# Stacked half-precision products for the sample states, chunk states ahead of the exponent differences, and key copies ahead of the weight split in a hybrid decoder step

## What is computed

```python
def hgrn2_block(s0, q, k, v, log_f):
    ...
    s_new = jnp.exp(b_last)[..., None] * s0 + jnp.einsum('bshk,bshv->bhkv', k * jnp.exp(b_last[:, None] - b), v)
    return s_new, o

def retention_block(s0, q, k, v):
    ...
    s_new = jnp.exp(c * log_gamma)[None, :, None, None] * s0 + jnp.einsum('bshk,bshv->bhkv', k * k_dec[None, :, :, None], v)
    return s_new, o
```

## Time and profile before

| | us |
|---|---|
| median of 3 runs | 1739.92 (1738.65 to 1740.34) |
| the profiled execution's own time | 1742.57 |
| its span, first to last instruction | 1741.0 |
| PE busy | 1567.8 (90%) |
| DVE busy | 904.5 (52%) |
| ACT busy | 654.0 (38%) |
| POOL busy | 154.3 (9%) |

### The profile page before, as it was taken

How to read it: one execution, slowest core, us unless ns; L and a number is a source line. 1 busy time by engine, 2 the same in 40 slices (tenths; PEclk the granted TensorE clock), 3 DMA queues, 4 the chain that set the end, 5 groups by cost and what they waited for, 6 DMA issues and landing times.

```text
span 1741.0 us, 31399 instructions
## 1 busy us (share of the span) xinstructions
PE 1567.8 (90%) x12107; PEld 1251.0 (72%) x12107; DVE 904.5 (52%) x1389; ACT 654.0 (38%) x920; POOL 154.3 (9%) x126
## 2 busy tenths in 40 slices
PE   4699999989699999999867999999886999999994
PEld 3477777767578888788755777777765888887883
DVE  4766644444565555533266665444356555553334
ACT  3645523332353334422155452333225443333213
POOL 2111111100200000000030111000002000000002
PEclk8799989988899999999978899999888999999997
DMA  6132222221123332233221224232031223322321
GB/s 192 46 90 77 75 75 75 74 74 55 57 73 97 96 96 77 70 93 95 82 66 51 74 74 111 57 88 78 27 97 48 88 83 96 96 81 74 97 66 51
DMA packets 175035, 138.05 MB, mean 79 GB/s; under 512 B 5064, under 2 KB 169192, under 8 KB 174776
## 3 DMA queue, kind: packets, MB, share of 16 engines
q1 hardware_dynamic: 168192, 113.46, 22.0%
q0 software_dynamic: 5408, 18.60, 3.8%
q10 hardware_dynamic: 1372, 5.16, 0.9%
HBM read 125.12 MB, written 12.07 MB: 79 GB/s over the span
## 4 chain that ended last, share of the span: by engine, by line
PE 77%; DVE 9%; ACT 6%; issue 4%; DVEq 2%; ACTq 1%; DMA 1%; SPq 0%
PE ACC L510 61%; PE SCR L624 2%; PE OT L632 2%; PE SCR L662 1%; ACT WH L830 1%; DVE X L1193 1%; PE OT L684 1%; PE SCR L545 1%; PE SCR L727 1%; DVE Z L1222 1%; DVE Fb L1206 1%; DVE WL L1153 1%; PE OT L600 1%; DVEq L1261 1%; PE OT L599 1%
## 5 line engine op out<-in xcount | busy, mean ns | idle before, releaser
L510 PE MATMUL ACC<-XH,WH 128*128 128x280 f16 x2432 | 502.6, 289 | 70.8 <-DVE XL L1196 43.1
L510 PE MATMUL ACC<-XL,WH 128*128 128x280 f16 x2432 | 502.4, 289 | 0.0
L510 PE MATMUL ACC<-XH,WL 128*128 128x280 f16 x2432 | 501.6, 289 | 0.0
L510 PEld LDWEIGHTS ACC<-XH,WH 128*128 128x128 f16 x2432 | 238.7, 101 | 153.0 <-DVE XL L1196 45.6
L1153 DVE SCALAR_TENSOR_TENSOR WL<-stage,WH 128x2048 f16<-128x2048 f32 (+1 forms) x116 | 245.9, 2120 | 182.0 <-ACT WH L830 170.2
L510 PEld LDWEIGHTS ACC<-XL,WH 128*128 128x128 f16 x2432 | 243.3, 100 | 58.6
L510 PEld LDWEIGHTS ACC<-XH,WL 128*128 128x128 f16 x2432 | 243.3, 100 | 58.0
L830 ACT ACTIVATE WH<-stage 128x2048 f16<-128x2048 f32 (+1 forms) x116 | 204.8, 1766 | 103.7 <-PE ACC L510 86.9
L510 PE MATMUL ACC<-shared,WH 128*128 128x280 f16 x1408 | 225.2, 283 | 0.2
L510 PEld LDWEIGHTS ACC<-shared,WH 128*128 128x128 f16 x1408 | 137.6, 98 | 30.8 <-issue 0.8
L510 PE MATMUL ACC<-shared,WL 128*128 128x280 f16 x704 | 141.5, 283 | 0.0
(11 more groups left out here) (238 smaller groups left out, 1791.4 us busy)
## 6 DMA issues: line engine op xcount, KB each, us to landing
stage<-in_w_in_dram SPq DMA_DIRECT2D x64, 512.0 KB, 5.3
stage<-in_w_a_dram SPq DMA_DIRECT2D x44, 512.0 KB, 4.3
stage<-in_w_b_dram SPq DMA_DIRECT2D x44, 512.0 KB, 4.8
stage<-in_w_down_dram SPq DMA_DIRECT2D x32, 384.0 KB, 3.3
stage<-in_w_down_dram SPq DMA_DIRECT2D x32, 320.0 KB, 3.7
out_dram<-shared POOLq DMA_DIRECT2D x16, 512.0 KB, 3.9
stage<-in_w_o_dram SPq DMA_DIRECT2D x16, 512.0 KB, 3.9
shared<-in_state_hgrn_dram POOLq DMA_DIRECT2D x8, 512.0 KB, 5.7
```

What stands on the lines that cost most here:

```text
L510: last = mm(ACC[:, acc, h, 0:HALF], lhs, x[:, xk + k, h * HALF:(h + 1) * HALF], start=begin, stop=end)
```

## The change

It does three things. First, the sample rows of keys and values are split into a float16 high part and a rest, and the three products high·high, high·rest and rest·high are stacked along the 96 rows of one float16 matmul: the three copies of the 32 sample columns are made ahead of the transposes (a broadcast copy of `KE` on DVE, a second read of the values on ACT), the transposes yield 96 rows, ACT writes all in float16 (`KV3`) and a float32 copy of the values (`VTS`) for the output product, and DVE puts the rest into 32 rows of the keys and 32 of the values (`low_sample_rows`). `VX` has 96 rows in float16. Second, DVE's chunk states (`b()`) come ahead of the exponent differences. Third, in the groups that carry a retention head ACT runs the head's first stage (`a()`) ahead of the weight split, and in the output projection ahead of the output gate.

```diff
-        VX = sb("VX", [TS, DEC_BATCH, P])
-        KVTS = sb("KVTS", [TS, 2, P])
+        VX = sb("VX", [TS3, DEC_BATCH, P], F16)
+        KV3 = sb("KV3", [TS3, 2, P], F16)
+        VTS = sb("VTS", [TS, P])
...
-                pool.wait_ge(tok_ready, hh + 1)
-                nc.gpsimd.tensor_tensor(VX[:, :, :], KVTS[:, 1:2, :].to_broadcast([TS, DEC_BATCH, P]), bcast(seqm[0:TS, :], P),
+                pool.wait_ge(kv_low, hh + 1)
+                nc.gpsimd.tensor_tensor(VX[:, :, :], KV3[:, 1:2, :].to_broadcast([TS3, DEC_BATCH, P]), bcast(seqm[0:TS3, :], P),
                                         ALU.mult).then_inc(vx_ready, 1)
...
-                mm(SCR[:, bank, :], KVTS[:, 0, :], VX[:, 4 * n:4 * n + 4, :].rearrange("p b v -> p (b v)"),
+                mm(SCR[:, bank, :], KV3[:, 0, :], VX[:, 4 * n:4 * n + 4, :].rearrange("p b v -> p (b v)"),
                    start=True, stop=True).then_inc(scr_full, 1)
...
             def read_acc(buf, c, tile, done):
                 act.wait_ge(acc_full, 1 + tile + 1)
-                f(halves(buf[:, 0:T]), ACC[:, c, :, 0:HALF], ACT.Copy, scale=INV_W).then_inc(acc_read[c], 1)
+                last = f(halves(buf[:, 0:T]), ACC[:, c, :, 0:HALF], ACT.Copy, scale=INV_W)
+                if buf is V:
+                    last = f(twice(V), ACC[:, c, 1:2, HALF - TS:HALF].to_broadcast([P, 2, TS]), ACT.Copy, scale=INV_W)
+                last.then_inc(acc_read[c], 1)
...
-                f(KVTS[:, :, :], SCR[0:TS, 0, 0:2 * P].rearrange("p (n v) -> p n v", n=2), ACT.Copy).then_inc(scr_read[0], 1)
+                f(KV3[:, :, :], SCR[0:TS3, 0, 0:2 * P].rearrange("p (n v) -> p n v", n=2), ACT.Copy)
+                f(VTS[:, :], SCR[0:TS, 0, P:2 * P], ACT.Copy).then_inc(kv_high, 1)
                 act.drain().then_inc(tok_ready, 1)
...
+                if b is not None:
+                    a()
                 split_hi(1, j, (acc_full, 1 + tile))
                 if output_squares is not None:
                     out_gate(hh - 1)
-                if a is not None:
+                if a is not None and b is None:
                     a()
...
+                a, b, _, c, d = rt_stages(l, HEADS - 1)
+                a()
                 out_gate((l + 1) * 2 * HEADS - 1)
...
+            def low_sample_rows(hh, at, decay):
+
+                keys, values = (slice(2 * TS, TS3), KV3[2 * TS:TS3, 0, :]), (slice(TS, 2 * TS), KV3[TS:2 * TS, 1, :])
+                dve.wait_ge(kv_high, hh + 1)
+                if decay is None:
+                    tt(keys[1], SCR[keys[0], 0, at:at + P], keys[1], ALU.subtract)
...
+                tt(values[1], SCR[values[0], 0, at + P:at + 2 * P], values[1], ALU.subtract).then_inc(scr_read[0], 1)
+                dve.drain().then_inc(kv_low, 1)
...
                 tt(QD[:, 0:T], Q[:, 0:T], E[:, 0:T], ALU.mult)
+                nc.vector.tensor_copy(twice(KE), KE[:, TP:T].unsqueeze(1).to_broadcast([P, 2, TS]))
                 dve.drain().then_inc(ew_ready, 1)
...
                 for job in RT_JOBS:
+                    if job is RT_JOBS[1]:
+                        low_sample_rows(hh, 2 * P, p)
                     full, _ = scr.job(bank)
...
+                hgrn_rows = (lambda: low_sample_rows(hh - 1, 0, None)) if steps else None
                 if kind == 0:
-                    hg_gate(l, head, tile)
-                    hg_exponents(l, head)
+                    hg_gate(l, head, tile, hgrn_rows)
                     if b is not None:
                         b()
+                    hg_exponents(l, head)
...
                     if after_hgrn:
 
+                        hgrn_rows()
                         dve.wait_ge(tok_ready, hh)
```

More of the change, by code:

```diff
@@ L143, in const_tables @@
     put("mask32", causal)
-    put("seq", tok[:, None] // DEC_SEQ == np.arange(DEC_BATCH)[None, :])
+    put("seq", np.tile(tok[:, None] // DEC_SEQ == np.arange(DEC_BATCH)[None, :], (3, 1)))
     log_g = np.log1p(-np.exp2(-5.0 - np.arange(HEADS)))
@@ L218, in hybrid_decoder_step @@
         Fb, T1, T2, T3, B, Q, QS, QD, KE, E, V, G = (
-            sb(n, [P, T + 2]) for n in ("Fb", "T1", "T2", "T3", "B", "Q", "QS", "QD", "KE", "E", "V", "G"))
+            sb(n, [P, T + (2 * TS if n in ("KE", "V") else 2)]) for n in ("Fb", "T1", "T2", "T3", "B", "Q", "QS", "QD", "KE", "E", "V", "G"))
         at = [0]
@@ L328, in bcast, with twice @@
             return ap.unsqueeze(2).to_broadcast([ap.shape[0], ap.shape[1], n])
+        def twice(t):
+            return t[:, T:T + 2 * TS].rearrange("p (a t) -> p a t", a=2)
         def level_halves(n, src=None):
@@ L577, in transposes @@
                         for i, src in enumerate(sources):
-                            last = nc.tensor.transpose(SCR[0:TS, bank, i * P:(i + 1) * P], src[:, TP:T], ident)
+                            last = nc.tensor.transpose(SCR[0:TS3, bank, i * P:(i + 1) * P], src[:, TP:TP + TS3], ident)
                     last.then_inc(scr_full, 1)
@@ L629, in sample_output @@
                 cols_ = OT[:, 1, TP - SPLIT:REST]
-                mm(cols_, KVTS[:, 1, :], PTSS[:, :], start=True, stop=False, skip_group_check=True)
+                mm(cols_, VTS[:, :], PTSS[:, :], start=True, stop=False, skip_group_check=True)
                 for b in range(DEC_BATCH):
@@ L1064, in _ @@
                     group(l, p + HEADS + 1, p + 1, 1, rt_stages(l, p))
+                a, b, _, c, d = rt_stages(l, HEADS - 1)
+                a()
                 out_gate((l + 1) * 2 * HEADS - 1)
-                for stage_ in rt_stages(l, HEADS - 1):
-                    if stage_ is not None:
-                        stage_()
+                b()
+                c()
+                d()
                 full, _ = scr_cin(l).job(0)
@@ L1196, in norm_apply, with hg_gate @@
                         tt(XL[:, m - 2, :], X[:, m - 2, :], XH[:, m - 2, :], ALU.subtract).then_inc(x_ready, 1)
-            def hg_gate(l, p, tile):
+            def low_sample_rows(hh, at, decay):
[3 more added lines that the diff above has]
+                    tt(keys[1], SCR[keys[0], 0, at:at + P], keys[1], ALU.subtract)
+                else:
+                    stt(out=keys[1], in0=SCR[keys[0], 0, at:at + P], scalar=tab[keys[0], ds(cols["k_dec_s"][0] + decay, 1)],
+                        in1=keys[1], op0=ALU.mult, op1=ALU.subtract)
+                tt(values[1], SCR[values[0], 0, at + P:at + 2 * P], values[1], ALU.subtract).then_inc(scr_read[0], 1)
+                dve.drain().then_inc(kv_low, 1)
+            def hg_gate(l, p, tile, low_rows=None):
                 n = l * HEADS + p
@@ L1203, in hg_gate @@
                 dve.drain().then_inc(f_ready, 1)
+                if low_rows is not None:
+                    low_rows()
                 dve.wait_ge(lnf_parts, n + 1)
```

11 lines of the change are left out of this document (7 added, 4 removed).

## The result

The change makes the kernel slower: 1761.42 us median (1758.76 to 1763.27), against 1740.13 for the kernel before on the same chip, a ratio of 1.0122 with a 95% interval of 1.0104 to 1.0139. The forecast was 1734, with 1722 to 1750 as its range. The profiled execution's span is 1758.8 us (before 1741.0), the mean granted clock 0.925 (before 0.931), and PE is busy 1553.9 us instead of 1567.8: it has less to do and takes longer.

A forecast was written before the change was run, and what follows sets the result against it. PE, busy nine tenths of the span, was taken as the bound. Terms 11.6 − 1.2 − 4.8 − 9.6 − 1.1 − 2.5 + 1.6 = −6.0 against 1742.57 gave 1736.6; the median 2.65 lower gave 1734, range 1722 to 1750.

The forecast's parts named there:

- The gate's wait: At the fourth tile's start in six HGRN2 groups, PE would wait some 6 us for ACT's query copy.
- behind the gate the clock decides: After PE's wait at the fourth tile, half speed would lose 2.1 us a group, bounds 0 and 2.7.
- slower by the clock: Rival: half speed after the fourth-tile wait lasts well into the next head, 5.1 us lost; 1749 us, chance 0.20.
- The gate's delay: HGRN2 groups: the fourth tile, waiting for the query copy, would start 0.8 us later than at 159.20.
- The first groups: First HGRN2 group with a head, each layer: 0.8 − 1.4 each, −1.2 us for two, half speed being long already.
- The last HGRN2 head: In the first retention group: shorter products and less half speed save 2.4 us, between 1.5 and 3.2; −4.8 for two.
- Retention: Four retention groups: shorter products and 1.15 of the 1.86 us wait saved, −9.6 us, plus −2.5 for half speed.
- The output projection: Second score product later behind DVE's output gate, 1.4 us lost, 1.28 won, perhaps longer half speed: +0.8, twice +1.6.
- POOL: HGRN2 groups: VX starts 0.7 us later; DVE's gate addition still ends with POOL's second operation, making the scan 0.65 later.
- the query is not late: Rival, HGRN2 groups: differences and exponentials run beside the states, −29 instead of +10; 1695 us, chance 0.07.
- retention keeps only the product: Rival, retention groups: ACT's copies or DVE's subtractions take 1.2 us longer, the wait's gain goes, +7; 1741 us, chance 0.17.
- both additions first: Rival: DVE's gate addition and subtraction pass between VX and L423, scan 1.0 us earlier, −9; 1725 us, chance 0.06.

The follow-up runs named there:

- dense restart: Changed kernel with later chunk outputs, sample outputs and mean squares moved in HGRN groups 1 to 3, so large float16 products follow the query-copy wait: 1752.84 us, ratio 1.0084.
- last kernel: Kernel with differences ahead of states, later output gate and GpSimd's decay before VX, but chunk states put ahead of exponent differences again: 1738.48 us, ratio 1.0004.
- fastest kernel: Changed kernel with exponent differences ahead of chunk states, output projection's masks and subtractions ahead of its output gate, and GpSimd's decay ahead of VX: 1694.72 us, ratio 0.9744.
- differences first: Changed kernel with DVE's exponent differences ahead of the chunk states again, as before the change: 1726.92 us, ratio 0.9938.
- query first: Changed kernel with ACT reading the query's projection out of its accumulator ahead of the exponentials in every HGRN group: 1740.17 us, ratio 1.0004.
- filled: Changed kernel with 56 more products of 212 columns ahead of the fourth tile in HGRN groups 1 to 3 of both layers: 1739.96 us, ratio 0.9999.

## Why the prediction was wrong

**The mechanism held, the size of one term did not.** The gate's wait was foreseen in place, cause and length (some 6; 5.55), and the query copy in the scan's wake (10.2 us behind it). The step that failed is the one "behind the gate the clock decides": half speed there was bounded by 0 and 2.7 us lost and put at 2.1, and it is 6.4. Four times the 4.3 us between the two are 17 us, three times the gain that was forecast. The bounds came from rows chosen by the length of the wait ahead (1.86, 2.45, 4.50). But behind 153.69 and behind 386.23 PE goes on with other work than behind the gate. The row 951.5 to 961.7 was the one with the chunk outputs at half speed, and the text used it only for a rival. Nor did the length of the wait bound anything in the kernel before. The row at 344.0 with 3.3 us at half speed stands behind a wait of 1.84 us, just under the 1.86 that left the clock at 1.00. And the sample-state products of the first groups had the 2.45 us of the earlier trace rows ahead of them:

```profile
343.26 0.28 PE L653 MATMUL SCR<-tab,KE 128*16 128x128 f32 x1 [1.84 <-ACT shared L960]
110.90 3.00 PE L624 MATMUL SCR<-VX,KVTS 32*128 32x512 f32 x4 [2.47 <-DVE shared L1347]
950.49 2.96 PE L624 MATMUL SCR<-VX,KVTS 32*128 32x512 f32 x4 [2.46 <-DVE shared L1347]
```

```profile
111.90:118.30 6.40, 6.40 (x24) 4.07 (x24) 4.34 (x9) 6.01 (x9) 0.60 (x1) 0.50 0.03 12
```

So three waits of 2.45 to 2.47 us, ahead of the same products, were followed by 3.2, 6.4 and 10.2 us at half speed. The rival that used the row at 951.5, "slower by the clock" (1749, chance 0.20), is what happened, and even its 5.1 was short: with the 16 four-column products in the stretch, 3.58 us at half speed, PE got through 12.8 us of work before the clock rose. Filling the wait took 21.5 us back, so the clock is shown as the cause and not only argued. The dense restart took 8.6 back, so the kind of work at the restart bears on how long half speed lasts; that it alone sets the length is not shown, and the first groups and the last kernel speak against it.

The signs of being right came (waits of 5.53 to 5.95 us at six gates, an addition that ends with POOL, retention groups 2.3 to 4.0 us shorter; the two old waits shrank, though not to zero), and the time was missed all the same. None of them tested how long half speed lasts behind the gate. The 7.2 us of the rival did, and groups 2 and 3 passed it with over 12.

The Trainium skill (TensorE: Matmul & The Clock Gate, section on HAM oscillation) describes that PE falls back to half clock after a wait and starts its next work cold, each time anew. The gates of groups 2 and 3 agree; how long it stays cold was read here from rows only.

**The gate's delay** was 1.22 and not 0.8: 0.08 more in the scan and 0.33 more with the states (0.27 of issue ahead of them), which the sum had left out. A small error beside the other.

**The first groups** were given −0.6 each, on the argument that half speed is long there already. In the second layer that is near (−0.2); in the first it is +3.6. The two periods are nearly the same after, 49.60 and 49.28 us, each with a wait of 5.9 us and more at the gate and a second stretch at half speed behind it. They differed before, 46.03 and 49.45: half speed lasted 6.4 us in the first layer, and 10.2 us and once more 3.4 in the second. The prediction took the second layer's row for both.

**The last HGRN2 head** brought 1.4 and not 2.4, just under the lower bound of 1.5. With POOL's decay out of the way, in the fastest kernel, the same group has −5.1 and −5.3. But kernels that leave the decay in its place and this group's code as it is have anything from −1.2 (differences first, first layer) to −3.8 (query first), so POOL's part in the missing 1.0 is not separated.

**Retention** was right as a sum (−12.7 for −12.1). PE and ACT in the group of the earlier trace rows, kernel after:

```profile
316.98 0.28 PE L660 MATMUL SCR<-tab,KE 128*16 128x128 f32 x1
...
319.65 0.71 PE L669 MATMUL SCR<-QD,KE 128*128 128x264 f32 x2 [0.76 <-DVE KV L1224]
```

```profile
315.78 1.14 ACT L971 ACTIVATE shared<-SCR,tab 128x128 f32<-128x128 f32 x4 [0.58 <-issue]
...
319.13 1.91 ACT L837 ACTIVATE WH<-stage 128x2048 f16<-128x2048 f32 x1 [0.34 <-issue]
```

The wait of 1.86 is gone and 0.76 for the subtractions stands in its place, as worked out (0.7). The split behind the copies is hidden, as it said: PE's waits for the weights' rest are 21.3 us in 4 times, 21.4 before.

**The output projection**, PE in the kernel after, beside the earlier trace rows:

```profile
393.56 0.28 PE L660 MATMUL SCR<-tab,KE 128*16 128x128 f32 x1 [1.90 <-ACT shared L971]
...
400.02 1.25 PE L669 MATMUL SCR<-QD,KE 128*128 128x264 f32 x2 [5.27 <-DVE KV L1224]
```

The wait of 4.50 became 1.90 and 5.27; the reason of the term, DVE's output gate ahead of the masks, held: with that gate later the longest wait there is 1.2. That its size came near (+0.8, measured +1.2 and +1.0) is partly luck: the row takes in all up to the next mark, and kernels with the same code there (differences first, query first, filled, dense restart) have from −2.0 to +3.5 in it.

**POOL.** The addition was to end with POOL's second operation, and it did: asked at 148.29 during `VX`, it ended at 151.12, behind L430's end at 150.51. By the rule of the Trainium skill that the prediction weighed (SBUF — State Buffer, section "SBUF: two separate sides") it could have slipped in as `VX` ended; the trace shows that it waited through both. What the prediction did not see is that this was the larger lever: the 1.46 us that the addition loses in the kernel before stood in the earlier trace rows, and moving the decay is worth 13 us there.

**Not borne out** were the rivals "the query is not late" (the wait of 5.55 stands), "retention keeps only the product" (0.76 in the place of 1.86) and "both additions first" (2.83).

## What to carry to other kernels

When an edit turns several short waits of TensorE into one long one, price what runs behind it at half clock. Take the price from rows with the same kind of work behind the wait, not from the wait's length, and let its bounds span all of them: here the same products ran at half clock for 6.8 to 13.6 us behind waits of 4.2 to 6 us, and large products in their place brought that to 4.2 to 6.4. Before two pieces of work on one engine swap places, ask which of them the next accumulator read hangs on; here 34 to 44 us hung on two calls. And where a two-input operation takes three times its usual time, look at what GpSimd does in that moment: work that it can do at any time belongs elsewhere.

## What the runs showed of the hardware

- TensorE's clock fell while PE was shown as busy: to 0.51 at 165.6 in the filled kernel and at 173.5 in the one with the dense restart, both times behind 16 products of four columns (1.95 us) and with no wait since the gate. It does not always: behind the same 16 products at 162.26 in the kernel before, and at 218.08 in the dense restart, it stays at 1.00.
- After waits of 4.18 and 5.55 us with the same small products behind them, 12.86 and 12.77 us of work ran at half speed; after 5.55 us with large products, 2.9. But after 5.93 us with the small products it was 4.2, and after two waits of 4.78 us in one kernel 13.1 and 4.1: neither the wait nor the work behind it fixes the length.
- A VectorE addition of two SBUF inputs that asked during the first of two GpSimd operations in a row ended only behind both (2.83 us instead of 0.74).
- GpSimd's multiplication of 1024 columns took 1.89 us in float16 with 96 rows, the same as in float32 with 32.
